# A two-layer decoder step on one core: x turned by products with diagonals of its row factors, and two more value units split into halves

## What is computed

```python
def rmsnorm(x, g):
    xf = x.astype(jnp.float32)
    y = xf * lax.rsqrt(jnp.mean(xf * xf, axis=-1, keepdims=True) + RMS_EPS) * g.astype(jnp.float32)
...
    q, k, v, qi, ki, wi = jnp.split(a @ w_in, ATTN_SPLITS, axis=-1)
...
    s = jnp.einsum('bqhd,bsd->bqhs', qi, ki, preferred_element_type=jnp.float32)
    score = jnp.einsum('bqhs,bqh->bqs', jax.nn.relu(s), wi.astype(jnp.float32)) * IDX_SCALE
    _, idx = lax.top_k(score, topk)
```

## Time and profile before

| | |
|---|---|
| median of 3 runs | 592.01 us (591.72 to 592.43) |
| the profiled execution | 592.18 us, its span 590.4 us |
| busy, of the span | PE 98%, PEld 85%, DVE 77%, ACT 63%, POOL 38% |
| the chain that ended last | PE 92%, DVE 3%, POOL 1%, ACT 1% |
| read from and written to memory | 108.83 MB and 3.86 MB, 191 GB/s over the span |

### The profile page before, as it was taken

How to read it: one execution, slowest core, us unless ns; L and a number is a source line. 1 busy time by engine, 2 the same in 40 slices (tenths; PEclk the granted TensorE clock), 3 DMA queues, 4 the chain that set the end, 5 groups by cost and what they waited for, 6 DMA issues and landing times.

```text
span 590.4 us, 12747 instructions
## 1 busy us (share of the span) xinstructions
PE 579.4 (98%) x5015; PEld 502.8 (85%) x5015; DVE 453.6 (77%) x904; ACT 369.7 (63%) x629; POOL 226.8 (38%) x230
## 2 busy tenths in 40 slices
PE   7999999999999999999999999999999999999995
PEld 7888889888888888888888888888888888888885
DVE  4899996666897778787778898789878777885542
ACT  6985566676765666575555788856756566654322
POOL 4241466713354544551000112273644555432220
PEclk9999999999999999999999999999999999999998
DMA  9959694329766766678997952065766666879602
GB/s 264 263 137 278 184 339 133 108 80 324 209 200 194 198 195 195 197 226 244 259 264 216 239 170 73 1 179 172 207 193 199 192 195 199 233 220 240 175 7 74
DMA packets 205420, 113.28 MB, mean 192 GB/s; under 512 B 5561, under 2 KB 202217, under 8 KB 205337
## 3 DMA queue, kind: packets, MB, share of 16 engines
q1 hardware_dynamic: 203169, 106.33, 63.9%
q0 software_dynamic: 1680, 5.79, 2.8%
q10 hardware_dynamic: 512, 0.35, 0.2%
HBM read 108.83 MB, written 3.86 MB: 191 GB/s over the span
## 4 chain that ended last, share of the span: by engine, by line
PE 92%; DVE 3%; POOL 1%; ACT 1%; issue 1%; DVEq 0%; ACTq 0%; POOLq 0%
PE acc L1538 25%; PE acc L1535 25%; PE acc L1541 25%; PE acc L1506 2%; PE acc L1726 1%; PE acc L1728 1%; PE acc L1727 1%; PE misc L1897 1%; PE acc L1561 1%; DVE w_lo L997 1%; PE misc L1663 1%; POOL hT L1930 1%; ACT w_hi L593 1%; PE misc L1642 1%; PE misc L1626 1%
## 5 line engine op out<-in xcount | busy, mean ns | idle before, releaser
L1535 PE MATMUL acc<-aH,w_hi 128*128 128x264 f16 (+1 forms) x886 | 244.5, 276 | 0.8 <-DVE work L1310 0.7
L1538 PE MATMUL acc<-aL,w_hi 128*128 128x264 f16 (+1 forms) x886 | 244.5, 276 | 0.0
L1541 PE MATMUL acc<-aH,w_lo 128*128 128x264 f16 (+1 forms) x886 | 244.5, 276 | 0.0
L997 DVE SCALAR_TENSOR_TENSOR w_lo<-stage,w_hi 128x1024 f16<-128x1024 f32 (+1 forms) x155 | 205.7, 1332 | 30.4 <-ACT w_hi L593 29.9
L593 ACT ACTIVATE w_hi<-stage 128x1024 f16<-128x1024 f32 (+1 forms) x155 | 171.1, 1109 | 32.4 <-PE acc L1541 25.2
L1535 PE MATMUL acc<-zH,w_hi 128*128 128x264 f16 x384 | 106.0, 276 | 0.0
L1538 PE MATMUL acc<-zL,w_hi 128*128 128x264 f16 x384 | 106.0, 276 | 0.0
L1541 PE MATMUL acc<-zH,w_lo 128*128 128x264 f16 x384 | 106.0, 276 | 0.0
L1538 PEld LDWEIGHTS acc<-aL,w_hi 128*128 128x128 f16 (+1 forms) x886 | 88.1, 99 | 13.5
L1535 PEld LDWEIGHTS acc<-aH,w_hi 128*128 128x128 f16 (+1 forms) x886 | 86.8, 98 | 14.5 <-issue 1.5
L1541 PEld LDWEIGHTS acc<-aH,w_lo 128*128 128x128 f16 (+1 forms) x886 | 88.1, 99 | 12.6
(11 more groups left out here) (421 smaller groups left out, 951.7 us busy)
## 6 DMA issues: line engine op xcount, KB each, us to landing
stage<-in_w_ffn_up SPq DMA_DIRECT2D x88, 512.0 KB, 4.7
stage<-in_w_ffn_down SPq DMA_DIRECT2D x32, 704.0 KB, 5.7
stage<-in_w_attn_in SPq DMA_DIRECT2D x22, 512.0 KB, 6.6
stage<-in_w_rec_in SPq DMA_DIRECT2D x16, 512.0 KB, 4.9
stage<-in_w_attn_out SPq DMA_DIRECT2D x8, 512.0 KB, 3.8
stage<-in_w_rec_out SPq DMA_DIRECT2D x8, 512.0 KB, 3.8
area<-in_w_attn_in SPq DMA_DIRECT2D x4, 512.0 KB, 4.6
area<-in_x_prompt SPq DMA_DIRECT2D x2, 512.0 KB, 4.6
```

The source lines that it names most:

```text
L997: v.scalar_tensor_tensor(low, stage[:, place_in_line(u) % 4, 0:n, 0:cols], WSCALE, high, ALU.mult, ALU.subtract).then_inc(lo_done, 1)
L1535: t_.matmul(out, high[:, c, :], xH[:, x0 + c, :], start=first and c == 0, stop=False)
L1538: t_.matmul(out, high[:, c, :], xL[:, x0 + c, :], start=False, stop=False)
L1541: ins = t_.matmul(out, low[:, c, :], xH[:, x0 + c, :], start=False, stop=last and c == n - 1)
```

## The change

At the start there are three parts with a root each: tile 0, tile 1 and the samples. Tile 1's squares are shared, half of the columns on ScalarE and half on VectorE. Instead of scaling the rows of x and transposing them, VectorE makes a 128 x 128 diagonal of each part's row factors (`row_factor`), and TensorE multiplies the raw x by it (`turn_x`). The warm-up is 8 products instead of 14. `hi(0)` and `lo(0)` move behind the second block of `aH` and `aL`. Three small loads of the page table move from ScalarE's queue into SyncE's. The diagonals are reused where ScalarE made them in step 16.

In the middle, `RAW_V` shrinks to units 15 and 16, so that units 13 and 14 are split, in steps 9 and 10. `turn_picked` moves into unit 15, `sample_dots` from steps 15, 16, 16, 17 to 16, 17, 18, 19, `sl_turned` from unit 20 to 21, `turn_weights` and what hangs on it from 22 to 23, and `sample_values` from units 23 and 24 to 24 and 25.

```diff
-RAW_V = U_V[2:6]
+RAW_V = U_V[4:6]
...
-WARM = 14
+WARM = 8
...
             for u in range(3):
                 load_in(u)
+            sp.dma_start(ptc[:], a["page_table"].rearrange("s g -> (s g)").unsqueeze(1).to_broadcast([2 * NS, 8]),
...
-            act.wait_ge(xs_in, 16)
-            nc.scalar.activation(scratch[0:NS, 1024:2048], xsmp, ACT.Square, accum_out=ss[0:NS, 2:3]).then_inc(ss_act, 1)
             act.wait_ge(x_in[0], 16)
-            nc.scalar.activation(scratch[:, 0:1024], xtok[:, 0, :], ACT.Square, accum_out=ss[:, 0:1]).then_inc(ss_act, 1)
+            nc.scalar.activation(scratch[:, 0:D], xtok[:, 0, :], ACT.Square, accum_out=ss[:, 0:1]).then_inc(ss_act, 1)
+            act.wait_ge(ss_act, 1)
+            nc.scalar.activation(rms[:, 0:1], ss[:, 0:1], ACT.Sqrt, bias=epsc[:, 0:1], scale=1.0 / D).then_inc(rms_root, 1)
+            act.wait_ge(x_in[1], 16)
+            nc.scalar.activation(scratch[:, D:D + D // 2], xtok[:, 1, D // 2:D], ACT.Square, accum_out=ss[:, 1:2]).then_inc(ss_act, 1)
...
-            nc.scalar.activation(xtok[:, 0, :], xtok[:, 0, :], ACT.Copy, scale=r0tok[:, 0:1]).then_inc(xn0, 1)
-            hi(0)
...
-                if c == 3:
+                if c == 1:
                     act.wait_ge(xg_done, 1)
                     nc.scalar.activation(aH[:, :, TP:T], xg[:], ACT.Copy).then_inc(xs_split, 1)
+                    hi(0)
...
+            def row_factor(n, rows_, t):
+
+                dve.wait_ge(rms_root, n)
+                v.reciprocal(r0tok[rows_, t:t + 1], rms[rows_, t:t + 1]).then_inc(r0tok_done, 1)
+                dve.wait_ge(r0tok_done, n)
+                v.tensor_scalar(rdiag[rows_, t, rows_], ident[rows_, rows_], r0tok[rows_, t:t + 1], None, ALU.mult).then_inc(rdiag_done, 1)
...
+            def turn_x(t):
+
+                pe.wait_ge(rdiag_done, 1 if t == 0 else 3)
+                for c in range(DC):
+                    ins = t_.matmul(misc[:, c // 2, c % 2 * TP + t * P:c % 2 * TP + t * P + P], xtok[:, t, c * P:(c + 1) * P],
+                                    rdiag[:, t, :], start=True, stop=True)
+                    if t and c % 2:
+                        ins.then_inc(x_turned, 1)
+
+            turn_x(0)
             pe.wait_ge(nrm_in, 16 * 3)
...
             ins.then_inc(s_turned, 1)
+            turn_x(1)
...
-                if 15 <= u < 17:
-                    sample_dots(u - 15)
+                if u == 16:
+                    sample_dots(0)
...
-                if 16 <= u < 18:
-                    sample_dots(u - 14)
-                if u == 20:
+                if 17 <= u < 20:
+                    sample_dots(u - 16)
+                if u == 21:
...
-                    elif u == 14:
-                        between = lambda i: turn_picked() if i == 8 else None
                     elif u == 15:
-                        between = lambda i: spread_queries() if i == 4 else None
-                    elif u == 22:
+                        between = lambda i: spread_queries() if i == 4 else turn_picked() if i == 8 else None
+                    elif u == 23:
                         between = lambda i: turn_weights() if i == 8 else None
```

80 lines of the change are left out of this document (34 added, 46 removed).

## The result

The changed kernel takes 604.96 us, median of 6 runs (602.87 to 605.8), beside 592.15 us (6 runs, 591.72 to 592.68) for the kernel before on the same chip: ratio 1.0209, 95% interval 1.0191 to 1.0228. That is 12.8 us slower, where I had said 4.3. The profiled execution took 604.99 us; its span is 603.0 us, 12.6 us more than before.

A forecast was written before the change was run, and what follows sets the result against it. TensorE was taken as the bound, with no delay given back; 1.55 (start) - 1.74 (value units) + 2.7 (wait at v2) + 1.75 (later waits) = +4.3 us, forecast 596.3 us, own range 595.0 to 597.4, whole range 593.6 to 598.4.

The forecast's parts named there:

- What bounds the kernel: Whole kernel: TensorE, busy 579.4 of 590.4 us; what it loses or wins in the first 120 us stays to the end.
- The two value units, -1.74: Units 13 and 14: split instead of raw, 2.70 us each for 3.57, saving TensorE 1.74 us.
- The wait at v2, +2.7: Ahead of unit 15: two lower halves on VectorE delay v2 to 65.25 us, so TensorE stands 2.7 us.
- turn_picked in unit 15: Unit 15: its result comes at about 69.2 us instead of 64.0, making VectorE 5.2 us late from there.
- Later waits, +1.75: TensorE waits behind unit 21's logits (+0.5), in unit 23 for the scores (+1.1) and at the first probabilities (+0.15).
- my rival that the later waits are not there: Units 16 to 21: VectorE catches up, leaving +2.5 us, 594.5 us; chance 0.22.
- The start, +1.55: Unit 0: first product at 14.9 us instead of 13.35, as its halves come onto the path; bounds +0.6 and +3.6.
- the case of the higher level: Start: TensorE at its high clock from 7.05 us, tile 0 done at 8.8 us; the start's lower bound, +0.6.
- the one of slow turning: Start: the low clock lasts and TensorE turns x more slowly, up to 598.2 us; chance 0.10.
- the one of four records for a product: Start: an f32 product costs four records instead of two, +2.2 us, given as 598.3 us; chance 0.02.
- The page-table loads: Start, SyncE's queue: they delay the third unit load and rotation tables by at most 2.1 us and cost nothing.
- the margin that holds: Turn of v2: v2 is kept before 62.57 us and no wait follows, given as 592.0 us; chance 0.10.

The follow-up runs named there:

- pool_v_later: Kernel before with units 13 and 14 split, lower halves on GpSimd, turn_picked late in unit 14, value gathers held until unit 17 is done: 592.27 us, ratio 1.0003.
- busy_at_v2: The changed kernel with ten filler products on TensorE between unit 14 and the turn of v2: 604.79 us, ratio 1.0215 to the kernel before.
- lo_before_picked: The changed kernel with VectorE's lower half of unit 18 made ahead of its wait for the picked rows: 600.83 us, ratio 1.0151 to the kernel before.
- dots_later_alone: Kernel before with only sample_dots, the scores, sl_turned, turn_weights and sample_values moved later as in the change: 596.20 us, ratio 1.0070.
- start_alone: Kernel before with only the changed start; the four raw value units and every step of the middle as before: 595.66 us, ratio 1.0066.
- samples_turned: Kernel before with the changed start, unit 0's halves made earlier, and samples turned by identity transposes without their row factors: 592.90 us, ratio 1.0009.

## Why the prediction was wrong

- **What bounds the kernel.** Right that nothing behind the change gives a delay back. What I left out is how full the change's own stretch is: I read stretches from 120 us on, and here only single rows. DMA share 1.02 and VectorE at 98% stood in one more stretch.
- **The two value units, -1.74.** Right: 0.86 us for each in pool_v_later.
- **The wait at v2, +2.7.** Right in place, cause and size: v2 kept at 65.25 + 2.37 = 67.62 us by my sum, 67.60 measured, wait 2.6. What I left out is the clock behind it, +1.7 us; I weighed the clock for the start alone. In busy_at_v2, where TensorE did not stand still, the clock did not fall there. The Trainium skill, TensorE: Matmul & The Clock Gate, "What's actually happening", says that the lower level is the default and activity releases it; the profiles of the change (0.50 behind the wait) and of busy_at_v2 (1.00 with filler) agree, but lo_before_picked kept 1.00 behind the same wait without filler, so standing still is not the whole cause.
- **turn_picked in unit 15.** This is the step of the prediction that failed. I had it 5.2 us late (72.80 us measured, with the low stretch in it) and followed it only into VectorE's small steps up to `sample_dots`. Behind it stand also `gix`, the gathers, and `lo(18)`, which frees the stage for unit 22's load: the issue of eight gathers and four loads was moved, and I put that at nothing. In the change the runs showed in its place a load of unit 23 that took 13.6 us for 6.1, and behind it 4.4 us of wait at k1's turn and some 1.6 of clock. Alone the step cost 4.3 us; in its profile about half of the waiting is behind the loads and half by VectorE's delay, which reached k0's turn through the rotation of unit 17.
- **Later waits, +1.75.** The mechanism exists: alone it costs 4.2 us, in dots_later_alone, with 1.2 us at `sl_turned` where I had 0.5, and six waits where I summed three. But in the change neither of the places I named waits: behind k1's turn TensorE has only 0.41 us at 108.92 and 0.65 us at 133.52. So for the changed kernel my rival that the later waits are not there came out, most likely for a reason I had not seen: the larger wait ahead of them gives VectorE time to catch up.
- **The start, +1.55.** Mis-sized: 2.2 to 2.4 us at unit 0, 3.5 us in the median of start_alone. The halves on the path were right in kind (1.4 of it at the first product). The samples' products, priced at twice a transpose (1.0 us), take 1.9 us, and the products of tile 0 end at 9.46 us, where the case of the higher level had 8.8. That level came at 6.27 us; it was my lower bound, +0.6, so against that case the start is 1.8 us off, not 0.8. Of the rivals for the start, the one of slow turning did not occur in this profile, but in that of samples_turned it did; the one of four records for a product fell: the trace has two.
- **The page-table loads.** No run moves them alone, so their price of nothing is not shown; TensorE's delay stays at 2.33 to 2.37 us from unit 0 to unit 13, so none came up there.
- **Sums.** Two of the rivals' times are off by 0.2 us: 4.3 + 2.2 gives 598.5 us for the product of four records, and 1.55 - 1.74 gives 591.8 us for the margin that holds. Neither changes the forecast. The measured 604.96 us is outside the whole range, 593.6 to 598.4.
